# Four gate units by chunk at the start of a two-block kernel, and mixed inputs in tiles of their own

## The chip, the cores and the metric

The kernel runs on one core of a Trainium2 chip (trn2). The metric is the device time of one execution in microseconds (us), median of the runs shown.

## The reference, cut to what matters

Two blocks over 512 tokens of width 1024 in float32. The change touches the first stage of the first block: a norm, the token shift, six mixtures of a token with the one before it, and of these two large products (gate g and reads r, 1024 to 2048) and two small ones for the hidden layers of the low-rank parts (1024 to 64).

```python
h = rms_norm(x, a_norm)
xx = token_shift(h) - h
lerp = lambda j: h + xx * mu[j]
xr, xw, xk, xv, xa, xg = (lerp(j) for j in range(6))
r = xr @ w_in[0]
g = xg @ w_in[3]
hidden_w = jnp.tanh(xw @ w1)      # 64 wide
hidden_a = xa @ a1                # 64 wide
# silu(g) is used at the end of the block, r in its scan
```

Keys and values, k = xk @ w_in[1] and v = xv @ w_in[2], are products of the next stage, which needs their mixed inputs from this one.

## The kernel before, in words

Channels lie on the 128 partitions, the 512 tokens along the free dimension. The width of 1024 is eight chunks (DC), the inner width of 2048 sixteen tiles (IC). Exact float32 products are made from halves: every weight and every input is split into an upper part (type fp32r, a copy that rounds) and a lower part (the whole minus the upper one), and `products` (L140) makes three matmuls for each chunk: upper by upper, upper by lower, lower by upper. One output tile of 128 channels is called a unit here: 8 chunks by 3 matmuls of 512 columns, 24 matmuls. `lerp_phase` (L206 to L511) has 32 of them, N = 32: units 0 to 15 are the gate, 16 to 31 the reads. Unit n uses the PSUM bank 2 + n % 4 (JOBS = 4) and the slot n % 2 of a ring of two weights (RING = 2), each slot with raw, upper and lower part of 128 x 1024.

Each engine has its own program, in an order written out by hand, tied by semaphores:
- SP loads x, a piece of the constants, the parameters, two weights, the first hidden weights, the rest of the constants (L243 to L255), then weight after weight. The load of weight n waits until the slot's weight before it is split (L239). The second hidden weights wait for the first hidden product (L264). From unit 20 on SP also stores finished reads.
- ScalarE squares x for the norm, makes the upper half of each weight (`split`, L299), of each mixed input (`hi`, L304), and the part (1 - mu) h of the gate's and decay's mixtures (`kept`, L311). In the loop over units (L335) it waits for unit n, makes the upper half of weight n + 2, and takes the tanh of the bank (or copies it, for the reads).
- VectorE sums the squares (L463), makes the lower halves of the weights (`split`, L439, through L151), the normed h (L418), the mixed inputs (`whole` L443, `shifted` L421, `lerps` L427), their lower halves (`lo`, L453), and per gate unit the product of the bank and its tanh (L494), which frees the bank.
- GpSimd prepares eight small parameter tiles of 128 x 16 (L285) and, when the gate's inputs are done, the eight differences xx of neighbouring tokens (L288), 128 x 511 each.
- TensorE: units 0 and 1 run side by side chunk by chunk as the inputs appear (`pair_by_chunk`, L388), then unit 2, the first hidden product (`hiddens`, L393, 8 float32 products), unit 3, units 4 and 5, the second hidden product, units 6 to 15. Then units 16 and 17 by chunk, since the reads' mixed inputs are only made then, in the same tiles x_hi and x_lo that the gate used: ScalarE's first write of them waits for gate unit 15 (L308). Units 18 to 31 follow.

The order of VectorE ahead of its loop (L471 to L482): the gate's inputs chunk by chunk, eight one-column instructions for xx (L478), the lower halves of weights 2 and 3, the decay's eight mixed inputs (`lerps(0)`), and a wait for the first hidden product. The two hidden products read their mixed inputs from the gate's output tile (`tmp`, L215), so the gate's results can only be written after those are used. The mixed inputs of keys and values (e = 8 to 23) are made beside units 4 to 11, two chunks a unit (L499).

```python
            pair_by_chunk(0, 0)
            job(2)
            hiddens(0)
            job(3)
```

Of the kernel before, what the change touches and what calls it, by code (L numbers as in the profile page):

```python
# [163 lines left out]
def program(nc, ins, out):  # L164
    with ExitStack() as top:
# [16 lines left out]
        with ExitStack() as right:  # L182
# [13 lines left out]
            with ExitStack() as left:  # L196
                K["lerp"] = {n: pair(left, f"lerp_{n}", DC) for n in "kv"}
                K["r_all"] = nc.dram_tensor("r_all", (IC, P, T), F32).ap()
                K["hidden"] = sbt(left, "hidden", [P, T])
                lerp_phase(K)  # L200
                rwkv_phase(K)
# [4 lines left out]
def lerp_phase(K):  # L206
# [4 lines left out]
    with ExitStack() as ctx:  # L211
# [3 lines left out]
        tmp = [gate[:, 0:DC, :], gate[:, DC:2 * DC, :]]  # L215
        h = x
        x_hi, x_lo = K["pair"](ctx, "xg", DC)
        raw, w_hi, w_lo = (K["sbt"](ctx, "g_" + n, [P, RING, DC * P], t) for n, t in
                           (("raw", F32), ("hi", F32R), ("lo", F32R)))
        full = K["sbt"](ctx, "lerp_full", [P, 2, T])  # L220
# [6 lines left out]
        block = ctx.enter_context(nc.Block())  # L227
        mu = V["a_mu"].rearrange("p (j c) -> p j c", j=6)
# [4 lines left out]
        SPLIT = [(name, j) for name in "gkvr" for j in range(DC)]  # L233
        pairs = {"g": (x_hi, x_lo), "r": (x_hi, x_lo), **lerp}

        @block.sync
        def _(sp):
            def load(n):
                need(sp, S("wlo"), n - RING + 1)  # L239
                sp.dma_start(raw[:, n % RING, :], ins["w_g" if n < IC else "w_r"][n % IC])\  # L240
                    .then_inc(S(f"w{n % RING}"), 16)
# [8 lines left out]
            for n in range(RING):  # L250
                load(n)
# [9 lines left out]
            for n in range(RING, N):  # L261
                load(n)
                if n == JOBS:
                    sp.wait_ge(S("hid_mm"), 1)  # L264
                    sp.dma_start(wl[:, :, :], ins["lora1"][:, :, LORA:P]).then_inc(S("wl"), 16)
                if n >= IC + JOBS:
# [8 lines left out]
        def _(pool):  # L275
# [3 lines left out]
            for n, name in enumerate("gw"):  # L279
                pool.tensor_scalar(rest[:, n, :], mu[:, MU[name], :], -1.0, 1.0, ALU.mult, ALU.add)\  # L280
                    .then_inc(S("rest"), 1)
            for n, (name, a, b) in enumerate((("a_w0", 0.5, 0.0), ("a_a0", 0.5, 0.0), ("a_ka", 0.5, 0.0),
# [8 lines left out]
        def _(act):  # L291
# [7 lines left out]
            def split(n):  # L299
                act.wait_ge(S(f"w{n % RING}"), 16 * (n // RING) + 16)  # L300
                need(act, S("g_mm"), n - RING + 1)
                act.activation(w_hi[:, n % RING, :], raw[:, n % RING, :], ACT.Copy).then_inc(S("whi"), 1)  # L302

            def hi(e):  # L304
                name, j = SPLIT[e]
                act.wait_ge(S("lerp_full"), e + 1)
                if name == "r" and j == 0:
                    act.wait_ge(S("g_mm"), IC)  # L308
# [24 lines left out]
            for j in range(DC):  # L333
                kept(1, j)
            for n in range(N):  # L335
                act.wait_ge(S("g_mm"), n + 1)
                if n == IC - 1:
                    hi(3 * DC)
                    hi(3 * DC + 1)
                if n + RING < N:  # L340
                    split(n + RING)
                if n == 2:
                    act.wait_ge(S("hid_mm"), 1)
                    act.activation(hidden[0:LORA, :], bank[1][0:LORA, :], ACT.Tanh).then_inc(S("hid"), 1)
                if n == 6:
                    act.wait_ge(S("hid_mm"), 2)
                    act.activation(hidden[LORA:P, :], bank[1][LORA:P, :], ACT.Copy).then_inc(S("hid"), 1)
                if n < IC:
                    need(act, S("gate"), n - 1)
                    act.activation(thg[:, n % 2, :], bank[2 + n % JOBS][:, :], ACT.Tanh, scale=0.5).then_inc(S("thg"), 1)  # L350
                    if n >= JOBS and n < JOBS + DC:
                        hi(DC + 2 * (n - JOBS))
                        hi(DC + 2 * (n - JOBS) + 1)
# [7 lines left out]
                if n == IC - 1:  # L361
                    for e in range(3 * DC + 2, 4 * DC):
                        hi(e)

        @block.tensor
        def _(pe):
# [4 lines left out]
            def job(n, ks=range(DC)):  # L371
# [8 lines left out]
                at = n % RING  # L380
                m = products(pe, bank[2 + n % JOBS][:, :], w_hi[:, at, ks[0] * P:], w_lo[:, at, ks[0] * P:],
# [4 lines left out]
            def pair_by_chunk(n, first):  # L386

                for k in range(DC):  # L388
                    pe.wait_ge(S("lerp_lo"), first + k + 1)
# [12 lines left out]

            pair_by_chunk(0, 0)
            job(2)
            hiddens(0)
            job(3)
            for n in range(JOBS, IC):
                job(n)
                if n == JOBS + 1:
                    hiddens(1)  # L410
            pair_by_chunk(IC, 3 * DC)
            for n in range(IC + 2, N):
# [2070 lines left out]
```

## Time and profile before

| | us |
|---|---|
| runs shown | 2048.4, 2050.85, 2056.65 |
| median | 2050.85 |
| the profiled execution | 2047.91 |
| its span | 2045.9 |
| matmul time of TensorE in the span | 1886.3 (92%) |
| last matmul of `lerp_phase` starts at | 235.53 |

The profile describes one execution. Times in it count from the start of its span. Engines are named PE (TensorE matmuls), PEld (its weight loads), DVE (VectorE), ACT (ScalarE), POOL (GpSimd) and SP (SyncE, which issues the DMAs). PEclk is the share of the full clock that TensorE was granted.

### The profile page before, as it was taken

Reading aid. Unit: us, or ns where it says so; the run is one execution under the profiler, and the core shown is the slowest. Engines: PE = TensorE matmul, PEld = TensorE weight load, DVE = VectorE, ACT = ScalarE, POOL = GpSimd, SP = SyncE. Lnnn points to the kernel's source line nnn. Section 1 sums busy time; section 2 is a strip of 40 time slices with the busy share of each in tenths; the row PEclk is TensorE's granted clock in tenths of the full one; section 3 lists DMA queues with packets and bytes.
Section 4 is the critical chain, followed back from the end, with each engine's and each line's share of the span. In section 5 each row is a group of like instructions: output and inputs, shape, how many; then the busy total and the mean of one; then the engine's idle time right before and its main releaser. Section 6 shows DMA issues by size and latency. Waiting matters only on the chain.

```text
span 2045.9 us, 43870 instructions
## 1 busy us (share of the span) xinstructions
PE 1886.3 (92%) x18912; PEld 1475.6 (72%) x18912; DVE 1253.5 (61%) x1787; ACT 884.2 (43%) x1368; POOL 294.1 (14%) x282
## 2 busy tenths in 40 slices
PE   4999779999999999899999999999888699999997
PEld 3677657676777767578888888887665478888885
DVE  6572168787777777544555554546557677787522
ACT  5342255646656466433222222334445354444321
POOL 3000033543535444400000000000000000000000
PEclk9999889999999999999999999999999799999998
DMA  3224311111111111143322223322110032223331
GB/s 123 78 83 139 104 42 45 42 45 41 46 30 42 45 42 39 43 151 97 103 94 94 102 93 101 96 93 73 52 42 21 21 114 98 97 93 103 91 93 64
DMA packets 51454, 154.15 MB, mean 75 GB/s; under 512 B 8512, under 2 KB 11072, under 8 KB 51264
## 3 DMA queue, kind: packets, MB, share of 16 engines
q1 hardware_dynamic: 51264, 151.35, 22.8%
q8 instruction: 151, 2.47, 0.5%
q14 instruction: 39, 0.32, 0.1%
HBM read 145.04 MB, written 6.29 MB: 74 GB/s over the span
## 4 chain that ended last, share of the span: by engine, by line
PE 51%; DVE 4%; ACT 1%; issue 0%; DMA 0%; DVEq 0%; ACTq 0%
PE bank L1653 15%; PE bank L1654 15%; PE bank L1652 15%; PE bank L1740 1%; PE bank L1741 1%; PE bank L1742 1%; DVE room L2364 0%; PE bank L1777 0%; DVE room L2331 0%; PE bank L1760 0%; PE bank L1821 0%; PE bank L1812 0%; PE bank L1723 0%; PE bank L1788 0%; PE bank L1785 0%
## 5 line engine op out<-in xcount | busy, mean ns | idle before, releaser
L1859 ACT ACTIVATE w_hi<-raw 128x1024 fp32r<-128x1024 f32 (+2 forms) x195 | 197.8, 1015 | 499.5 <-PE bank L1654 457.0
L1652 PE MATMUL bank<-h_hi,w_hi 128*128 128x512 f32 x896 | 349.8, 390 | 0.0
L1654 PE MATMUL bank<-h_hi,w_lo 128*128 128x512 f32 x896 | 348.6, 389 | 0.0
L1653 PE MATMUL bank<-h_lo,w_hi 128*128 128x512 f32 x896 | 348.6, 389 | 0.0
L151 DVE TENSOR_TENSOR w_lo<-raw,w_hi 128x1024 fp32r<-128x1024 f32 (+2 forms) x202 | 236.2, 1170 | 155.2 <-ACT w_hi L1859 154.7
L1652 PEld LDWEIGHTS bank<-h_hi,w_hi 128*128 128x128 f32 x896 | 168.2, 188 | 35.7 <-issue 0.7
L1653 PEld LDWEIGHTS bank<-h_lo,w_hi 128*128 128x128 f32 x896 | 168.2, 188 | 35.5 <-issue 0.7
L1654 PEld LDWEIGHTS bank<-h_hi,w_lo 128*128 128x128 f32 x896 | 168.2, 188 | 34.9
L144 PE MATMUL bank<-xg_hi,g_hi 128*128 128x512 f32 x256 | 104.4, 408 | 21.6 <-DVE g_lo L151 11.8
L814 ACT ACTIVATE swapT<-invT 64x256 f32<-64x256 f32 x192 | 79.8, 415 | 83.3 <-DVE invT L1367 41.1
L1634 POOL TENSOR_SCALAR room<-room 128x512 f32<-128x512 f32 x4 | 3.5, 884 | 696.7 <-ACT room L1928 696.7
L145 PE MATMUL bank<-xg_lo,g_hi 128*128 128x512 f32 x256 | 102.8, 402 | 0.0
L146 PE MATMUL bank<-xg_hi,g_lo 128*128 128x512 f32 x256 | 102.7, 401 | 0.0
L151 DVE TENSOR_TENSOR g_lo<-g_raw,g_hi 128x1024 fp32r<-128x1024 f32 x32 | 40.7, 1276 | 91.5 <-ACT g_hi L302 91.5
L1652 PE MATMUL bank<-y_hi,w_hi 128*128 128x512 f32 x224 | 87.7, 391 | 2.3 <-PEq L134 1.3
L1000 PEld LDWEIGHTS bank<-inv,LA 64*64 64x64 f32 x2560 | 46.9, 134 | 59.4 <-issue 59.4
L1653 PE MATMUL bank<-y_lo,w_hi 128*128 128x512 f32 x224 | 88.9, 397 | 0.0
L1654 PE MATMUL bank<-y_hi,w_lo 128*128 128x512 f32 x224 | 88.4, 395 | 0.0
L1347 DVE TENSOR_TENSOR low<-bank,con 128x512 f32<-128x512 f32 x80 | 55.1, 689 | 45.0 <-PE bank L1000 44.9
L1352 DVE TENSOR_TENSOR invT<-invT,bank 128x512 f32<-128x512 f32 x80 | 55.1, 688 | 40.3 <-PE bank L1012 40.3
L144 PEld LDWEIGHTS bank<-xg_hi,g_hi 128*128 128x128 f32 x256 | 50.0, 195 | 39.5 <-DVE xg_lo L151 13.9
L1000 PE MATMUL bank<-inv,LA 64*64 64x64 f32 x2560 | 56.3, 224 | 23.6 <-DVE inv L1356 17.1
(389 smaller groups left out, 4301.3 us busy)
## 6 DMA issues: line engine op xcount, KB each, us to landing
raw<-in_w_conv SPq DMA_DIRECT2D x64, 512.0 KB, 3.2
raw<-in_w_up SPq DMA_DIRECT2D x44, 512.0 KB, 3.2
raw<-in_w_out SPq DMA_DIRECT2D x32, 512.0 KB, 3.8
raw<-in_w_in SPq DMA_DIRECT2D x20, 512.0 KB, 3.2
g_raw<-in_w_g SPq DMA_DIRECT2D x16, 512.0 KB, 3.2
g_raw<-in_w_r SPq DMA_DIRECT2D x16, 512.0 KB, 3.8
w_k<-in_w_k SPq DMA_DIRECT2D x16, 512.0 KB, 4.1
w_v<-in_w_v SPq DMA_DIRECT2D x16, 512.0 KB, 3.6
```

The lines of the kernel that those rows point to most:

```text
L144: pe.matmul(out, w_hi[:, w], x_hi[:, k, :], start=(first and n == 0), stop=False)
L145: pe.matmul(out, w_hi[:, w], x_lo[:, k, :], start=False, stop=False)
L146: m = pe.matmul(out, w_lo[:, w], x_hi[:, k, :], start=False, stop=(last and n == len(ks) - 1))
L151: return dve.tensor_tensor(lo, full, hi.bitcast(F32), ALU.subtract)
L814: act.activation(swapT[rows[1 - j], :, :], invT[rows[j], 1, :, :], ACT.Copy).then_inc(S("swap"), 1)
L1000: m = pe.matmul(X[h][rows[j ^ h], cols(b)], LA[rows[j], h, b, 0, :], inv[rows[j], h, b, :], start=True, stop=True)
L1347: dve.tensor_tensor(low[:, :, :, :], heads(0), over2(C["level_mask"][:, lv * HD:(lv + 1) * HD]), ALU.mult).then_inc(S("low"), 1)
L1352: up = dve.tensor_tensor(invT[:, :, :, :], invT[:, :, :, :], heads(half), ALU.add)
L1652: pe.matmul(to, whi, hi, start=begin, stop=False)
L1653: pe.matmul(to, whi, lo, start=False, stop=False)
L1654: last = pe.matmul(to, wlo, hi, start=False, stop=end)
L1859: act.activation(w_hi[:, g % RING, 0:width], raw[:, g % RAW, 0:width], ACT.Copy).then_inc(S("whi"), 1)
```

## The change

Units 0 to 3 run side by side by chunk: units 2 and 3 one chunk (LAG = 1) behind units 0 and 1. Their weights are loaded at the start. Those of units 2 and 3 lie in tiles `more` over the lower part of the values' input tiles (24 of 32 KB for each partition), with semaphores of their own; GpSimd makes their upper halves. The gate's mixed inputs lie in the keys' input tiles, the reads' in a pair `xr` of their own. The two hidden products' mixed inputs (`mixed_w`, `mixed_a`) lie over `xr`, no longer over the gate's output. The first hidden product comes after unit 5, the second after unit 7. The mixed inputs of reads, values and keys, in this order, are made beside units 8 to 19 (MIX = 8), two chunks a unit, and units 16 and 17 are ordinary units. On VectorE the decay's mixed inputs come ahead of the splits of weights 4 and 5, and the waits for the hidden products in its loop go.

```diff
-                K["lerp"] = {n: pair(left, f"lerp_{n}", DC) for n in "kv"}
+                K["lerp"] = {"k": pair(left, "lerp_k", DC)}
+                K["lerp_v_at"] = -(-nc.sbuf_base // 32) * 32
+                K["lerp"]["v"] = pair(left, "lerp_v", DC)
...
-        tmp = [gate[:, 0:DC, :], gate[:, DC:2 * DC, :]]
-        x_hi, x_lo = K["pair"](ctx, "xg", DC)
+        over = lambda name, at, shape, t: nc.alloc_sbuf_tensor_at(name, shape, t, offset=at)
+        r_at = -(-nc.sbuf_base // 32) * 32
+        pairs = {"g": lerp["k"], "r": K["pair"](ctx, "xr", DC), **lerp}
+        tmp = [over(f"mixed_{n}", r_at + 4 * DC * T * k, [P, DC, T], F32) for k, n in enumerate("wa")]
...
+        more = [over(f"g_{n}_more", K["lerp_v_at"] + 8 * DC * P * k, [P, 2, DC * P], t) for k, (n, t) in
+                enumerate((("raw", F32), ("hi", F32R), ("lo", F32R)))]
+        of = lambda n: [t[:, n - 2, :] for t in more] if n in (2, 3) else [t[:, n % RING, :] for t in (raw, w_hi, w_lo)]
+        MIX, LAG = 8, 1
...
+        weight = lambda n: f"w{n}" if n in (2, 3) else f"w{n % RING}"
+        loads = lambda n: 16 if n < JOBS else 16 * ((n - JOBS) // RING + 2)
...
-        SPLIT = [(name, j) for name in "gkvr" for j in range(DC)]
-        pairs = {"g": (x_hi, x_lo), "r": (x_hi, x_lo), **lerp}
+        SPLIT = [(name, j) for name in "grvk" for j in range(DC)]
...
             def load(n):
-                need(sp, S("wlo"), n - RING + 1)
-                sp.dma_start(raw[:, n % RING, :], ins["w_g" if n < IC else "w_r"][n % IC])\
-                    .then_inc(S(f"w{n % RING}"), 16)
+                if n >= JOBS:
+                    sp.wait_ge(S("wlo"), n - 3 if n < JOBS + 2 else n - 1)
+                sp.dma_start(of(n)[0], ins["w_g" if n < IC else "w_r"][n % IC]).then_inc(S(weight(n)), 16)
...
-            for n in range(RING):
+            for n in range(JOBS):
                 load(n)
...
-            for n in range(RING, N):
-                load(n)
-                if n == JOBS:
+            for n in range(JOBS, N):
+                if n == MIX:
                     sp.wait_ge(S("hid_mm"), 1)
                     sp.dma_start(wl[:, :, :], ins["lora1"][:, :, LORA:P]).then_inc(S("wl"), 16)
+                load(n)
...
+            for n in (2, 3):
+                pool.wait_ge(S(weight(n)), 16)
+                pool.tensor_scalar(of(n)[1], of(n)[0], 1.0, 0.0, ALU.mult, ALU.add).then_inc(S("whi_more"), 1)
...
             def split(n):
-                act.wait_ge(S(f"w{n % RING}"), 16 * (n // RING) + 16)
-                need(act, S("g_mm"), n - RING + 1)
-                act.activation(w_hi[:, n % RING, :], raw[:, n % RING, :], ACT.Copy).then_inc(S("whi"), 1)
+                act.wait_ge(S(weight(n)), loads(n))
+                need(act, S("g_mm"), n - 3 if n < JOBS + 2 else n - 1)
+                act.activation(of(n)[1], of(n)[0], ACT.Copy).then_inc(S("whi"), 1)
...
-                if name == "r" and j == 0:
-                    act.wait_ge(S("g_mm"), IC)
+                if j == 0 and name != "g":
+                    act.wait_ge(*{"r": (S("hid_mm"), 2), "v": (S("g_mm"), JOBS), "k": (S("g_mm"), IC)}[name])
...
+            split(JOBS)
+            split(JOBS + 1)
             for n in range(N):
                 act.wait_ge(S("g_mm"), n + 1)
-                if n == IC - 1:
-                    hi(3 * DC)
-                    hi(3 * DC + 1)
-                if n + RING < N:
+                if JOBS <= n < N - RING:
                     split(n + RING)
-                if n == 2:
+                if n == 6:
-                if n == 6:
+                if n == MIX:
-                    if n >= JOBS and n < JOBS + DC:
-                        hi(DC + 2 * (n - JOBS))
-                        hi(DC + 2 * (n - JOBS) + 1)
...
-                if n == IC - 1:
-                    for e in range(3 * DC + 2, 4 * DC):
-                        hi(e)
+                if MIX <= n < MIX + 3 * DC // 2:
+                    hi(DC + 2 * (n - MIX))
+                    hi(DC + 2 * (n - MIX) + 1)
...
-                at = n % RING
-                m = products(pe, bank[2 + n % JOBS][:, :], w_hi[:, at, ks[0] * P:], w_lo[:, at, ks[0] * P:],
+                _, hi, lo = of(n)
+                x_hi, x_lo = pairs["g" if n < IC else "r"]
+                m = products(pe, bank[2 + n % JOBS][:, :], hi[:, ks[0] * P:], lo[:, ks[0] * P:],
...
-            def pair_by_chunk(n, first):
-
-                for k in range(DC):
-                    pe.wait_ge(S("lerp_lo"), first + k + 1)
+            def two_by_chunk(n, k):
+                if k < DC:
+                    pe.wait_ge(S("lerp_lo"), k + 1)
                     for s in range(2):
                         job(n + s, [k])
...
-            pair_by_chunk(0, 0)
-            job(2)
-            hiddens(0)
-            job(3)
-            for n in range(JOBS, IC):
+            for k in range(DC + LAG):
+                two_by_chunk(0, k)
+                if k >= LAG:
+                    two_by_chunk(2, k - LAG)
+            for n in range(JOBS, N):
+                if n == IC:
+                    pe.wait_ge(S("lerp_lo"), 2 * DC)
                 job(n)
-                if n == JOBS + 1:
-                    hiddens(1)
-            pair_by_chunk(IC, 3 * DC)
-            for n in range(IC + 2, N):
-                job(n)
+                if n in (5, 7):
+                    hiddens((n - 5) // 2)
...
-                dve.wait_ge(S("whi"), n + 1)
-                split_lo(dve, w_lo[:, n % RING, :], raw[:, n % RING, :], w_hi[:, n % RING, :]).then_inc(S("wlo"), 1)
+                dve.wait_ge(*((S("whi_more"), n - 1) if n in (2, 3) else (S("whi"), n + 1 if n < 2 else n - 1)))
+                split_lo(dve, of(n)[2], of(n)[0], of(n)[1]).then_inc(S("wlo"), 1)
...
-            split(0)
-            split(1)
+            for n in range(JOBS):
+                split(n)
...
-            split(RING)
-            split(RING + 1)
             lerps(0)
-            dve.wait_ge(S("hid_mm"), 1)
+            split(JOBS)
+            split(JOBS + 1)
             for n in range(N):
-                if n == IC - 1:
-                    for e in (3 * DC, 3 * DC + 1):
-                        lo(e)
-                        whole(e + 2)
-                if RING <= n < N - RING:
+                if JOBS <= n < N - RING:
                     split(n + RING)
                 if n < IC:
-                    if n == IC // 2:
...
-                if n < 2:
-                    lerps(1, range(n * DC // 2, (n + 1) * DC // 2))
-                if JOBS <= n < JOBS + DC:
-                    e = DC + 2 * (n - JOBS)
+                if n in (JOBS, JOBS + 1):
+                    lerps(1, range((n - JOBS) * DC // 2, (n - JOBS + 1) * DC // 2))
+                if MIX <= n < MIX + 3 * DC // 2:
+                    e = DC + 2 * (n - MIX)
                     whole(e)
                     whole(e + 1)
                     lo(e)
                     lo(e + 1)
-                if n == IC - 2:
-                    whole(3 * DC)
-                    whole(3 * DC + 1)
-                if n == IC - 1:
-                    for e in range(3 * DC + 2, 4 * DC):
-                        lo(e)
-                        if e + 2 < 4 * DC:
-                            whole(e + 2)
```

## Rows read from the trace of the kernel before

**Rows 1.** The page: span, and TensorE's busy time.
```profile
span 2045.9 us, 43870 instructions
...
PE 1886.3 (92%) x18912; PEld 1475.6 (72%) x18912; DVE 1253.5 (61%) x1787; ACT 884.2 (43%) x1368; POOL 294.1 (14%) x282
```

**Rows 2.** Busy time by stretch; columns: length, each engine's (instructions), clock, DMA, GB/s.
```profile
21.10:25.10 4.00, 4.00 (x9) 3.14 (x10) 3.91 (x7) 2.48 (x4) 0.00 (x0) 1.00 0.00 0
25.10:37.00 11.90, 10.28 (x40) 6.74 (x38) 9.32 (x22) 7.85 (x13) 1.43 (x2) 1.00 0.00 0
42.70:49.75 7.05, 7.03 (x25) 5.43 (x25) 7.05 (x8) 0.00 (x0) 2.85 (x2) 0.80 0.24 74
62.50:64.60 2.10, 0.00 (x0) 0.00 (x0) 2.10 (x4) 1.54 (x2) 0.00 (x0) 1.00 0.01 4
64.60:72.10 7.50, 7.47 (x26) 5.95 (x27) 2.30 (x3) 0.00 (x0) 0.00 (x0) 0.77 0.43 140
...
139.10:155.40 16.30, 12.45 (x46) 9.80 (x47) 11.24 (x16) 6.25 (x10) 0.00 (x0) 0.90 0.10 33
155.40:165.30 9.90, 8.09 (x29) 6.17 (x29) 2.45 (x2) 2.98 (x4) 0.00 (x0) 0.83 0.52 159
165.30:236.00 70.70, 70.62 (x312) 58.15 (x310) 14.70 (x12) 19.17 (x26) 0.00 (x0) 1.00 0.41 123
```

**Rows 3.** Waits of TensorE in 0 to 285 us: total, times, longest.
```profile
PE bank L144 <- DVE g_lo L151: 11.8, 4, 5.5
PE bank L144 <- DVE xg_lo L151: 9.8, 6, 6.6
```

**Rows 4.** Timeline of TensorE; columns: start, us, engine, line, operation, operands, count.
```profile
21.10 0.79 PE L144 MATMUL bank<-xg_hi,g_hi 128*128 128x512 f32 x1 [6.63 <-DVE xg_lo L151]
...
49.73 7.08 PE L399 MATMUL bank<-gate,lora_w 128*64 128x512 f32 x16
```

**Rows 5.** Timeline of VectorE, 12 to 36 us.
```profile
12.34 2.38 DVE L151 TENSOR_TENSOR g_lo<-g_raw,g_hi 128x1024 fp32r<-128x1024 f32 x2
17.30 1.42 DVE L418 SCALAR_TENSOR_TENSOR x_in<-x_in,par,thg 128x512 f32<-128x512 f32 x2 [2.59 <-ACT thg L161]
...
20.96 0.75 DVE L423 SCALAR_TENSOR_TENSOR lerp_full<-x_in,par,lerp_full 128x511 f32<-128x511 f32 x1
...
23.03 0.74 DVE L423 SCALAR_TENSOR_TENSOR lerp_full<-x_in,par,lerp_full 128x511 f32<-128x511 f32 x1
...
35.40 0.57 DVE L478 TENSOR_SCALAR xx<-x_in 128x1 f32<-128x1 f32 x8
```

**Rows 6.** The gate's weights, their issue on SP, and the traffic then.
```profile
DMA to landing us min/median/max: 3.2/4.3/7.7
...
4.09 0.93 SPq L240 DMA_DIRECT2D g_raw<-in_w_g  x2
...
13.00:14.00 1.00, 1.00 (x2) 0.00 (x0) 1.00 (x2) 0.38 (x1) 1.00 (x2) 1.00 1.02 425
```

**Rows 7.** Durations (min/median/max ns): a GpSimd copy, and its small instruction.
```profile
L687 POOL TENSOR_SCALAR w_k_hi<-w_k x14: 1047/1057/1479, 294.4 to 762.9; 128x1024 fp32r<-128x1024 f32 x14
...
L285 POOL TENSOR_SCALAR mixpar<-par x8: 214/446/1188, 10.7 to 14.8; 128x16 f32<-128x16 f32 x8
```

**Rows 8.** GpSimd's differences and what met them on VectorE.
```profile
L288 POOL TENSOR_TENSOR xx<-x_in x8: 1038/1039/2022, 35.6 to 43.5; 128x511 f32<-128x511 f32 x8
...
42.59 2.06 DVE L151 TENSOR_TENSOR g_lo<-g_raw,g_hi 128x1024 fp32r<-128x1024 f32 x1
44.57 1.52 DVE L423 SCALAR_TENSOR_TENSOR gate<-x_in,par,gate 128x511 f32<-128x511 f32 x1
...
46.01 0.74 DVE L423 SCALAR_TENSOR_TENSOR gate<-x_in,par,gate 128x511 f32<-128x511 f32 x1
...
46.67 0.74 DVE L423 SCALAR_TENSOR_TENSOR gate<-x_in,par,gate 128x511 f32<-128x511 f32 x1
```

**Rows 9.** Timeline of ScalarE in unit 9.
```profile
101.12 1.06 ACT L302 ACTIVATE g_hi<-g_raw 128x1024 fp32r<-128x1024 f32 x1 [0.53 <-PE bank L146]
```

More of the change, by code:

```diff
@@ L478, in _ @@
                 dve.tensor_scalar(xx[:, j, 0:1], h[:, j, 0:1], -1.0, None, ALU.mult).then_inc(S("xx0"), 1)
-            split(RING)
-            split(RING + 1)
             lerps(0)
-            dve.wait_ge(S("hid_mm"), 1)
+            split(JOBS)
+            split(JOBS + 1)
             for n in range(N):
-                if n == IC - 1:
-                    for e in (3 * DC, 3 * DC + 1):
-                        lo(e)
-                        whole(e + 2)
-                if RING <= n < N - RING:
+                if JOBS <= n < N - RING:
                     split(n + RING)
                 if n < IC:
-                    if n == IC // 2:
-                        dve.wait_ge(S("hid_mm"), 2)
                     dve.wait_ge(S("thg"), n + 1)
```

## The prediction

> **What bounds the kernel now.** The page first: TensorE is busy for 92% of the 2045.9 us span [rows 1], so time lost on it counts, if no other engine is late. The change touches the first 236 us alone, so the next view is the busy time by stretch of that part [rows 2]. A unit is one of the 32 output tiles (16 of the gate, 16 of the reads), 24 matmuls. The last thirteen read units take 70.7 us with 312 matmuls, TensorE without a hole: 5.44 us a unit and 0.227 us a matmul. They end at 236.0. The rest of the stretch has holes. The waits of TensorE say on whom: 5.5 us at most and 11.8 us in all on the lower halves of the weights, 9.8 us on those of the inputs, of which 6.6 us is the wait for the first one [rows 3]. The timeline gives the fixed points: first unit matmul at 21.10 and the first product for a hidden layer, 7.08 us; the second is of the same size [rows 4].
>
> Losses against 24 x 0.2267 = 5.44 us a unit, from [rows 2]:
> - Two gate units by chunk: 21.1 to 37.0 is 15.9 us for 10.9 us of work, 5.0 lost. 1.9 of it is the slow start (9 matmuls in 4.0 us), 3.1 are waits for input chunks.
> - Before unit 2: 5.7 us of hole (37.0 to 42.7), then 7.05 us for the unit, 1.6 more than at full clock.
> - Before unit 4: 2.1 us of hole, then 7.5 us, 2.1 more than 5.44.
> - The first two read units: 16.3 us for 10.9, 5.4 lost.
> - Unit 18: 9.9 us from the end of that pair, 4.5 more than a unit.
>
> Slow start aside these make 3.1 + 7.3 + 4.2 + 5.4 + 4.5 = **24.5 us**. The granted clock is below 1 in the stretches behind the holes (0.80, 0.77, 0.83): part of them ran at 1.2 instead of 2.4 GHz. What came before each fall was a hole or a run of short holes.
>
> **What the change takes away.** (a) Units 0 to 3 run chunk by chunk, 12 matmuls a chunk: 12 x 0.227 = 2.72 us. VectorE gives a chunk every 2.07 us (20.96 to 23.03 [rows 5]). TensorE is the slower one, so the 3.1 us go. (b) Weights 2 and 3 are there from the start, so the hole before unit 2 goes with its cold part, 7.3 us. (c) The hidden product no longer stands between units 3 and 4 with its work on VectorE behind it; 4.2 us go, though something takes the place (below). (d) The reads' inputs have tiles of their own and are made beside units 8 to 11; the pair stage and the hole behind it go, 9.9 us. Unit 16 then waits only for a count reached four units earlier.
>
> **What it adds, at the start.** VectorE now does four weight splits before the norm, where it did two (12.34 to 14.72), and was then idle until 17.30 [rows 5]. The upper halves of weights 2 and 3 come from GpSimd, which is in this place for the first time. Landing: the second weight landed 7.7 us after its issue, which is 12.2 (issues from 4.09 on, 0.93 us for two). DMA moves about 400 GB/s there, so 512 KB more land every 1.3 us: 13.5 and 14.9 [rows 6]. GpSimd takes 1.05 us for the same operation on another weight, VectorE 1.2 us for its own, and one GpSimd instruction of 16 columns took up to 1.19 us instead of 0.21, in the time of VectorE's splits [rows 7]: the two take turns. So from 12.34 on: four VectorE splits of 1.17 start to start and two GpSimd copies of about 0.95 in turn, 4.7 + 1.9 = 6.6, end 18.9; plus 0.2 for the eight small parameter instructions which GpSimd had done by then and now does later. The norm starts at 19.1 to 19.2 instead of 17.30: **+1.9 us**. Ends: 0, if the copies run free (14.9 + 1.05 + 1.2 = 17.2), and 3.8, if a landing is 1 us later and the small instructions take their 0.1 to 0.3 each between VectorE's.
>
> **What it adds, before unit 4.** From here times are without the 1.9. TensorE is busy from 21.10: 9 matmuls to 25.1, 87 x 0.227 more: four units are done at 45.0. VectorE finishes the last input chunk at 35.5 and eight one-column instructions at 36.0 [rows 5]. Then, in its new order, it makes the eight mixed inputs of the first hidden product before the splits of weights 4 and 5. They stand exactly where GpSimd computes the eight differences (from 35.57, 1.04 us each alone). The trace shows what two such operations do to each other: a difference beside a split took 2.02, a split 2.06 instead of 1.2, and the one mixed input that met GpSimd 1.52 instead of 0.74. It started at 44.57 and the next at 46.01: 1.44 apart, against 0.67 alone (46.01 to 46.67) [rows 8]. Before, GpSimd had nearly finished when they came; now all eight meet it. 36.0 + 8 x 1.44 = 47.5. Behind them in VectorE's queue stand the splits of weights 4 and 5 (2.3 us) and the gate of unit 0 (0.7), which frees the bank: 50.5. TensorE waits 50.5 - 45.0 = **5.5 us**, and starts again at a low clock: +1.6 to +2.1 by the two cold units above, **1.8**. Ends of the hole: 0.8 if there is no collision (eight at 0.67 end at 41.4, but ScalarE's half of weight 4 needs unit 0's end, 3.4 us before 45.0; +1.1, two splits, a gate: 45.8), and 7 if a turn costs the sum of both.
>
> The Trainium skill, page "SBUF — State Buffer", section "Who interferes with whom", says that the pair of ports common to VectorE and GpSimd is locked for the whole instruction and the loser fully blocks. By that rule each turn would cost both durations, 1.04 + 0.74 = 1.78 us, and the hole would be 2.7 us longer than in my sum; the rows show 1.44, and the sum goes by them.
>
> **What costs nothing.** Four instead of two weights are issued at the start; the two more stand in front of the first hidden weights and constants in SP's queue, which are needed more than 30 us later. SP waits for the first hidden product before load 8: issued at the end of that product, landed some 4 us later, used by ScalarE after unit 6, 5.4 us later; everything behind it in the queue (load 9 on) is due a unit later still. If that cover went, unit 8 would be late, but the second hidden product and unit 7 stand before it, 12.5 us. The second set of mixed inputs stands beside units 4 and 5, needed after unit 7. The twelve units with input chunks (8 to 19) are what 4 to 11 were: ScalarE has 0.53 us left of 5.44 a unit [rows 9], and a weight may be 3 us late on top before TensorE notices. The values' inputs wait for unit 3, the keys' for unit 15: both long done. The end of the stage and all after it is untouched.
>
> **Sum.** 24.5 - 1.9 - 5.5 - 1.8 = 15.3 us. As a check: 23.0 start, 23.7 four units with the slow start, 5.5 hole, 1.8 cold, 28 x 5.44 = 152.3, 14.2 hidden: 220.5, against 236.0. The profiled execution took 2047.91 us (2.0 outside the span), so it would be 2032.6. The median shown lies 2.9 above that execution. I forecast the median, 2050.85 - 15.3 = **2035.5 us**.
>
> **Rivals.**
> 1. No collision: the eight mixed inputs run at 0.67. The hole is 0.8 and the clock stays: 24.5 - 1.9 - 0.8 = 21.8, 2029. Against it: the one sample that met GpSimd was slowed. For it: one sample only, beside the last of GpSimd's eight. Chance 0.11.
> 2. Full turns of 1.78 us: 2038. For it: 2.06 for a split beside a difference is near to the sum of 1.2 and 1.04; against it the 1.44. The skill's rule named above is this case. Chance 0.12.
> 3. Start and hole both at their dear ends and a further small stall, for instance unit 16 waiting for its inputs because they are not made ahead as the change says, which would give back the 5.4 us of the pair: saving 5 to 10, 2041 to 2046. Chance 0.14.
> 4. Slower: ScalarE's and VectorE's chain of a unit with two input chunks is 4.9 us of 5.44 now. If it grows past 5.44, each of twelve units is paced by it; from 6.7 us a unit on (15.3 / 12 = 1.3 more) the gain is gone, at 7.6 the kernel takes some 2061. Eight units show it at 4.9 without a stall, and GpSimd is silent there. Chance 0.03.
>
> **How the numbers follow.** The forecast has 0.60, its own range 2032 to 2039 (start 0.5 to 3, hole 4 to 7, run to run 2). The 8-in-10 range takes in rival 2 and most of 1 and reaches to the edge of 3: 2028 to 2041. A measurement of this kernel can tell about 0.5%, 10.3 us, from no change. Faster by more than that: forecast, rivals 1 and 2, 0.83. Same: rival 3, 0.14. Slower: 0.03.
>
> **What would show it.** The norm's first VectorE instruction near 19.2. From the first unit matmul no waits for inputs through four units, ending some 26 us later. Mixed inputs on VectorE from about 38, 1.4 us apart, each beside a GpSimd difference; then one TensorE hole of 5 to 6 us, released by VectorE's gate, and a few us at 1.2 GHz behind it. After that a unit every 5.44 us, with no hole at unit 16 or 18; the last ends near 220.5. I am wrong if that hole is under 2 or over 8 us, if the first matmul comes after 25, or if another hole opens from unit 5 on.

## The result, and the profile after

The changed kernel takes 2036.01 us (median of eight runs, 2032.24 to 2042.27), the kernel before 2051.64 us (eight runs, 2048.4 to 2056.65). The ratio is 0.9932 with a 95% interval of 0.9918 to 0.9947: 15.6 us less, where 15.3 us less had been forecast.

The page of the changed kernel says little; its span is only 6.6 us shorter than that of [rows 1], because its profiled execution was one of the longer of the eight (2041.11 us):

```profile
span 2039.3 us, 43871 instructions
...
PE 1888.7 (93%) x18912; PEld 1480.4 (73%) x18912; DVE 1260.3 (62%) x1787; ACT 883.0 (43%) x1366; POOL 298.2 (15%) x284
```

The stage that was changed has to be read by itself. Its end is the copy of the last read unit, in ScalarE's timeline: first the kernel before, then the changed one. It comes 15.49 us earlier.

```profile
235.96 0.60 ACT L360 ACTIVATE thg<-bank 128x512 f32<-128x512 f32 x1 [4.84 <-PE bank L146]
```

```profile
220.47 0.60 ACT L369 ACTIVATE thg<-bank 128x512 f32<-128x512 f32 x1 [4.84 <-PE bank L146]
```

Busy time by stretch of the changed kernel answers to [rows 2] (columns as there):

```profile
22.60:28.40 5.80, 5.80 (x14) 4.54 (x15) 5.67 (x9) 3.73 (x6) 0.00 (x0) 1.00 0.00 0
28.40:47.50 19.10, 19.09 (x84) 15.44 (x82) 17.59 (x27) 12.26 (x19) 10.45 (x8) 1.00 0.01 1
47.50:51.70 4.20, 0.00 (x0) 0.00 (x0) 4.20 (x5) 0.00 (x0) 0.70 (x1) 1.00 0.16 42
51.70:59.10 7.40, 7.34 (x25) 5.92 (x26) 1.80 (x3) 1.20 (x2) 0.00 (x0) 0.77 0.32 118
100.00:154.40 54.40, 54.40 (x242) 45.05 (x241) 43.94 (x59) 28.54 (x41) 0.00 (x0) 1.00 0.33 105
154.40:220.50 66.10, 66.03 (x292) 54.34 (x290) 16.62 (x16) 18.88 (x26) 0.00 (x0) 1.00 0.42 127
```

The rows show four units without a hole (98 records, with those at the edges), then one hole of 4.2 us, a unit of 7.4 us with a granted clock of 0.77, and, in the rows from 100 us on, a full TensorE to the end of the stage. Nothing is left of the read pair. The waits and the timeline of TensorE show that one hole and who ends it:

```profile
PE bank L144 <- DVE lerp_k_lo L151: 8.0, 1, 8.0
PE bank L144 <- DVE gate L496: 4.3, 1, 4.3
```

```profile
22.59 0.79 PE L144 MATMUL bank<-lerp_k_hi,g_hi 128*128 128x512 f32 x1 [8.05 <-DVE lerp_k_lo L151]
...
51.76 0.47 PE L144 MATMUL bank<-lerp_k_hi,g_hi 128*128 128x512 f32 x1 [4.27 <-DVE gate L496]
```

VectorE's timeline of the changed kernel, against [rows 5]: the norm begins at 18.80 instead of 17.30, behind two splits of 1.6 us each. The eight mixed inputs take 11.38 us, which is 1.42 us each, and the splits of weights 4 and 5 and the gate stand behind them:

```profile
15.69 3.19 DVE L151 TENSOR_TENSOR g_lo_more<-g_raw_more,g_hi_more 128x1024 fp32r<-128x1024 f32 x2 [0.94 <-POOL g_hi_more L294]
18.80 1.40 DVE L427 SCALAR_TENSOR_TENSOR x_in<-x_in,par,thg 128x512 f32<-128x512 f32 x2
...
37.37 11.38 DVE L432 SCALAR_TENSOR_TENSOR mixed_w<-x_in,par,mixed_w 128x511 f32<-128x511 f32 x8
48.67 2.35 DVE L151 TENSOR_TENSOR g_lo<-g_raw,g_hi 128x1024 fp32r<-128x1024 f32 x2
50.94 2.68 DVE L496 SCALAR_TENSOR_TENSOR gate<-thg,bank 128x512 f32<-128x512 f32 x4
```

GpSimd's timeline beside it: its eight differences take 11.15 us, from 37.05 to 48.2. In the kernel before they took 10.0 us, and in experiment 1 below, where next to nothing meets them, 8.0 us.

```profile
13.66 3.02 POOL L294 TENSOR_SCALAR g_hi_more<-g_raw_more 128x1024 fp32r<-128x1024 f32 x2 [2.85 <-DMA g_raw_more<-in_w_g]
...
37.05 11.15 POOL L301 TENSOR_TENSOR xx<-x_in 128x511 f32<-128x511 f32 x8 [15.16 <-DVE lerp_k_lo L151]
```

### The profile page after: what moved, and what is told of

Same layout as the page of the kernel before. It is cut to its first block, busy times and chain, and to the rows that moved or that the text cites. A ratio compares the mean times of both kernels' runs of the same rounds, so it can differ in the third digit from the quotient of the medians.

```text
span 2039.3 us, 43871 instructions
## 1 busy us (share of the span) xinstructions
PE 1888.7 (93%) x18912; PEld 1480.4 (73%) x18912; DVE 1260.3 (62%) x1787; ACT 883.0 (43%) x1366; POOL 298.2 (15%) x284
## 4 chain that ended last, share of the span: by engine, by line
PE 51%; DVE 4%; ACT 1%; issue 0%; DVEq 0%; ACTq 0%
PE bank L1647 15%; PE bank L1648 15%; PE bank L1646 15%; PE bank L1734 1%; PE bank L1736 1%; PE bank L1735 1%; DVE room L2358 0%; PE bank L1771 0%; DVE room L2325 0%; PE bank L1754 0%; PE bank L1815 0%; PE bank L1806 0%; PE bank L1717 0%; PE bank L1782 0%; PE bank L1779 0%
## 5 line engine op out<-in xcount | busy, mean ns | idle before, releaser
L151 DVE TENSOR_TENSOR g_lo<-g_raw,g_hi 128x1024 fp32r<-128x1024 f32 x30 | 36.6, 1224 | 81.4 <-ACT g_hi L315 81.4
L1006 PEld LDWEIGHTS bank<-invT,low 64*64 64x64 f32 x1280 | 45.1, 134 | 33.3 <-issue 33.3
L2090 DVE TENSOR_TENSOR x<-x,bank 128x512 f32<-128x512 f32 x32 | 21.9, 686 | 73.7 <-PE bank L1648 68.5
L315 ACT ACTIVATE g_hi<-g_raw 128x1024 fp32r<-128x1024 f32 x30 | 31.7, 1059 | 82.7 <-PE bank L146 82.7
L1006 PE MATMUL bank<-invT,low 64*64 64x64 f32 x1280 | 54.9, 223 | 10.4 <-DVE low L1341 10.4
```

The lines of the kernel that those rows point to most:

```text
L151: return dve.tensor_tensor(lo, full, hi.bitcast(F32), ALU.subtract)
L315: act.activation(of(n)[1], of(n)[0], ACT.Copy).then_inc(S("whi"), 1)
L1006: m = pe.matmul(X[h][rows[j], cols(TB + b)], low[rows[j ^ h], h, b, :], right, start=True, stop=True)
L2090: dve.tensor_tensor(x[:, n, :], x[:, n, :], bank[at + n % wide(tag)][:, :], ALU.add)\
```

## The experiments

The theory: TensorE sets the pace of the stage, VectorE's queue makes the one hole that is left, and it does so because the mixed inputs and GpSimd's differences take turns (when both are due, one waits while the other works). The effect of an edit is read from the end of the stage; the times of whole runs scatter by more than most of the effects (last part of this section).

**1. The mixed inputs later.** The eight mixed inputs of the decay are taken out from ahead of the splits.

```diff
-            lerps(0)
             split(JOBS)
             split(JOBS + 1)
             for n in range(N):
...
+                if n == JOBS - 1:
+                    lerps(0)
                 if n in (JOBS, JOBS + 1):
```

> The changed kernel, but the decay's eight mixed inputs are made on VectorE after the gate of unit 3, no longer ahead of the splits of weights 4 and 5. Theory (VectorE's queue, stretched by turns with GpSimd's differences, made the 4.3 us hole before unit 4 and the slow clock behind it): four units end at 47.5, the splits at 47.5 and the gate of unit 0 at 48.1, a hole of about 0.7 us, no fall of the clock; unit 4 starts 3.6 us earlier and takes 5.4 instead of 7.4 us. The stage's last unit ends near 214.9 instead of 220.5, the time is 5.6 us under the changed kernel (about 2030.5). Rival (the hole has another cause, weight 4 or the bank): the end stays at 220.5. Rival (the clock falls there whatever happens): the end is near 217.

Measured: median 2030.91 us, ratio to the kernel before 0.9907 (0.9887 to 0.9928). The stage ends at 215.24. TensorE and VectorE, timelines of this kernel:

```profile
48.17 0.47 PE L144 MATMUL bank<-lerp_k_hi,g_hi 128*128 128x512 f32 x1 [0.90 <-DVE gate L495]
```

```profile
47.35 2.69 DVE L495 SCALAR_TENSOR_TENSOR gate<-thg,bank 128x512 f32<-128x512 f32 x4
49.95 5.38 DVE L432 SCALAR_TENSOR_TENSOR mixed_w<-x_in,par,mixed_w 128x511 f32<-128x511 f32 x8
```

Busy time by stretch, unit 4 of this kernel:

```profile
48.20:53.70 5.50, 5.50 (x25) 4.56 (x26) 5.37 (x9) 1.12 (x2) 0.00 (x0) 1.00 0.41 138
```

The hole is 0.90 instead of 4.27 us, unit 4 starts 3.6 us earlier, and the clock did not fall: its stretch takes 5.5 us at a granted clock of 1.00. Neither weight 4 nor the bank had another cause for more than these 0.90 us. The same eight instructions take 5.38 us once the differences are done (GpSimd's end at 45.2 here). Both rivals fall. From the start of unit 4 to the end of the stage the changed kernel took 168.71 us and this one 167.07, so the fall of the clock costs 1.6 us there.

**2. The differences later.** VectorE's order stays, GpSimd waits.

```diff
-                pool.wait_ge(S("lerp_lo"), DC)
+                pool.wait_ge(S("lerp"), DC)
```

> The changed kernel, but GpSimd's eight differences wait for the decay's eight mixed inputs to be done, so that they no longer run side by side. Theory (the two engines take turns): the mixed inputs start 0.67 us apart instead of 1.42 and end near 42.8 instead of 48.8; the differences then meet the splits of weights 4 and 5, which take about 2.0 us each instead of 1.2; the gate of unit 0 ends near 50, the hole is about 2.5 us, the stage ends at 217 to 219. Rival (mixed inputs slow for another reason, such as ScalarE's half or TensorE's reading beside them): they keep 1.42 us, end stays at 220.5 or comes later.

Measured: median 2029.96 us, ratio 0.9905 (0.9874 to 0.9936), stage end at 214.94.

```profile
37.49 5.37 DVE L432 SCALAR_TENSOR_TENSOR mixed_w<-x_in,par,mixed_w 128x511 f32<-128x511 f32 x8
43.89 3.20 DVE L151 TENSOR_TENSOR g_lo<-g_raw,g_hi 128x1024 fp32r<-128x1024 f32 x2 [1.03 <-ACT g_hi L315]
```

Below are GpSimd's timeline of this kernel, and the durations (min/median/max ns) of the mixed inputs, first in the changed kernel, then in this one:

```profile
42.94 10.03 POOL L301 TENSOR_TENSOR xx<-x_in 128x511 f32<-128x511 f32 x8 [20.95 <-DVE mixed_w L432]
```

```profile
L432 DVE SCALAR_TENSOR_TENSOR mixed_w<-x_in,par,mixed_w x8: 1266/1521/1522, 37.4 to 47.2; 128x511 f32<-128x511 f32 x8
```

```profile
L432 DVE SCALAR_TENSOR_TENSOR mixed_w<-x_in,par,mixed_w x8: 741/744/746, 37.5 to 42.1; 128x511 f32<-128x511 f32 x8
```

In the same place, with ScalarE and TensorE at work beside them as before, the mixed inputs start 0.67 us apart: it was GpSimd. The two splits now meet the differences and take 3.20 us instead of 2.35, less than the 4.0 expected. The end came earlier than the 217 to 219 expected, because the hole was 1.74 us instead of 2.5 and the clock did not fall behind it.

**3. Two units, then two.** Only TensorE's order is undone.

```diff
-            for k in range(DC + LAG):
+            for k in range(DC):
                 two_by_chunk(0, k)
-                if k >= LAG:
-                    two_by_chunk(2, k - LAG)
+            for k in range(DC):
+                two_by_chunk(2, k)
```

> The changed kernel with its four weights, but TensorE takes units 0 and 1 by chunk and then units 2 and 3 by chunk. Theory (the restart before unit 4 is set by VectorE's queue at 51.7, not by TensorE): the first pair ends at 38.5, the second at 49.4 instead of 47.5, the hole shrinks from 4.3 to 2.3 us and unit 4 starts at 51.7 as before; the stage ends at 219.5 to 220.5, no difference in time. Rival (running four side by side is itself what brings the gain): the stage ends 2 to 3 us later, 222.5 to 223.5.

Measured: median 2035.2 us, ratio 0.9929 (0.9902 to 0.9956), stage end at 220.73. The waits for input chunks are back (9.5 us in all, of which 8.3 is the wait for the first chunk). The four units end at 49.84 instead of 47.49, the hole is smaller by nearly as much, and unit 4 starts when VectorE lets it:

```profile
PE bank L144 <- DVE lerp_k_lo L151: 9.5, 4, 8.3
PE bank L144 <- DVE gate L496: 2.2, 1, 2.2
```

```profile
52.04 0.60 PE L144 MATMUL bank<-lerp_k_hi,g_hi 128*128 128x512 f32 x1 [2.21 <-DVE gate L496]
```

The end moves by 0.3 us, as does the first matmul (22.87 instead of 22.59); two executions of the changed kernel differ by 1.5 us (run 8 below). The rival, an end 2 to 3 us later, falls. In the changed kernel the side by side order brings nothing that shows. What is gained ahead of unit 4 must then come from the weights that are ready and the hidden product that has moved; neither was tried alone.

**4. The reads' part alone.** Built on the kernel before: only the tiles, the order of the mixed inputs and the read units are changed.

```diff
-        SPLIT = [(name, j) for name in "gkvr" for j in range(DC)]
-        pairs = {"g": (x_hi, x_lo), "r": (x_hi, x_lo), **lerp}
+        SPLIT = [(name, j) for name in "grvk" for j in range(DC)]
+        MIX = 8
+        pairs = {"g": lerp["k"], "r": (xr_hi, xr_lo), **lerp}
...
-            for n in range(JOBS, IC):
+            for n in range(JOBS, N):
+                if n == IC:
+                    pe.wait_ge(S("lerp_lo"), 2 * DC)
                 job(n)
...
-            pair_by_chunk(IC, 3 * DC)
-            for n in range(IC + 2, N):
-                job(n)
...
```

> The kernel before with one part of the change: the gate's mixed inputs in the keys' tiles, the reads' in a pair of their own, made beside units 8 to 11, and units 16 and 17 as ordinary units. Start, weights and hidden products as before. Theory (this part is worth the 5.4 us of the pair stage and the 4.5 us of unit 18): the stage ends near 226.1 instead of 236.0, time 9.9 us under the kernel before, near 2041.7. Rival (the holes only move, because inputs or weights come late beside units 12 to 19): the stage ends at 230 or later.

Measured: median 2041.95 us, ratio 0.9965 (0.9949 to 0.9981), stage end at 224.82, 11.1 us under [rows 2]'s 236.0. Busy time by stretch in this kernel, the hole before unit 4, unit 4, and the time of some eighteen units from 120 us on:

```profile
62.70:64.90 2.20, 0.05 (x2) 0.00 (x1) 2.20 (x4) 1.54 (x2) 0.00 (x0) 1.00 0.01 4
64.90:70.35 5.45, 5.45 (x24) 4.48 (x25) 2.27 (x3) 0.00 (x0) 0.00 (x0) 1.00 0.55 192
...
120.00:219.30 99.30, 99.30 (x440) 82.23 (x439) 47.58 (x57) 38.92 (x54) 0.00 (x0) 1.00 0.40 126
```

There is no hole from 120 on. From the end of unit 15 to the end of the stage this kernel takes 86.95 us (137.87 to 224.82) and the kernel before 96.76 (139.20 to 235.96): 9.8 us, where 9.9 were expected. The rest of the 11.1 is chance. The hole before unit 4 is the one of [rows 2], 2.15 us in the waits of both, but the clock fell behind it there and not here. So this part carries 9.8 of the 15.5 us, and all that happens before the end of unit 15 carries 5.7. The median is only 7.2 us under that of the kernel before in the same series (2049.16 us), and the profiled execution was the fastest of nine, so the 9.8 us rest on the stage and not on the time of whole runs.

**5. Two, then two, with a free VectorE.** The edits of 1 and 3 together.

> Both edits of the first and third experiment: the decay's mixed inputs after the gate of unit 3, and TensorE takes units 0 and 1, then units 2 and 3. Theory (with VectorE's queue free, TensorE's own order decides): the first pair is again paced by VectorE until 38.6, the second ends at 49.5, unit 4 starts at 49.6 without a hole instead of 48.2, the stage ends at 216.2 to 216.8 instead of 215.2: side by side is worth 1 to 1.5 us, and only here. Rival (the order never matters): 215.2 again. Rival (it is worth the whole 3.1 us of waits): 218.

Measured: median 2031.0 us, ratio 0.9906 (0.9881 to 0.993), stage end at 216.68 instead of 215.24; there is no wait for the gate in this kernel. The order is worth 1.4 us, as expected (one profile of this kernel), and only once VectorE's queue does not hide it. The median of the whole run does not show it.

**6. The splits of weights 2 and 3 behind the second chunk**, on top of 1, to win back the start.

```diff
-            for n in range(JOBS):
+            for n in range(2):
                 split(n)
...
                 lo(j)
+                if j == 1:
+                    split(2)
+                    split(3)
```

> The first experiment's kernel (decay's mixed inputs after the gate of unit 3), and on VectorE the splits of weights 2 and 3 stand behind the second input chunk, no longer ahead of the norm. Theory (the two splits and GpSimd's copies are what delays the start by 1.5 us; TensorE, slower than VectorE by 0.65 us a chunk, has room for 2.4 us of them later): the norm starts at 17.3, the first unit matmul at 21.1, units 2 and 3 start near 25.8, a wait of at most 1 us for the third chunk; four units end at 45.5 to 46.5, the stage ends at 213 to 214.3 instead of 215.2, time near 2029.5. Rival (the delay only moves from the start to units 2 and 3): the first matmul at 21.1 but the end at 215.2. Rival (the holes at chunk 2 bring the slow clock back): the end at 216 or later.

Measured: median 2030.24 us, ratio 0.9902 (0.9884 to 0.9921), but the stage ends at 216.43, later than in 1. VectorE's timeline shows the norm back at 17.31, and what happened further on:

```profile
17.31 1.47 DVE L427 SCALAR_TENSOR_TENSOR x_in<-x_in,par,thg 128x512 f32<-128x512 f32 x2 [2.32 <-ACT thg L161]
...
43.32 3.66 DVE L151 TENSOR_TENSOR g_lo<-g_raw,g_hi 128x1024 fp32r<-128x1024 f32 x2 [5.02 <-ACT g_hi L315]
```

```profile
47.70:55.00 7.30, 7.28 (x25) 5.86 (x26) 7.05 (x11) 1.16 (x2) 0.17 (x1) 0.77 0.21 72
```

The second fence is the stretch of unit 4. TensorE is 1.5 us ahead, so the splits of weights 4 and 5 come earlier and now meet the differences (3.66 instead of 2.36 us), the hole is 2.19 us, and the clock falls behind it. The second rival of the expectation holds (the slow clock is back), for a hole in another place than it named. The start itself is won back: the first unit matmul comes at 21.16, so the two splits were what had delayed it.

**7. Both meetings avoided.** Edit 6 without edit 1, and the differences behind the splits of weights 4 and 5.

```diff
-                pool.wait_ge(S("lerp_lo"), DC)
+                pool.wait_ge(S("wlo"), JOBS + 2)
```

> The changed kernel with two edits: the splits of weights 2 and 3 stand behind the second input chunk, and GpSimd's differences wait for the splits of weights 4 and 5, so that they meet neither the mixed inputs nor these splits. Theory (the start's delay and the two meetings of VectorE and GpSimd are all that is left between this stage and a full TensorE): norm at 17.3, first unit matmul at 21.1, mixed inputs 0.67 us apart, the splits 1.2 us each, a hole of about 0.9 us before unit 4 and no slow clock behind it; the stage ends at 212.5 to 214, 6.5 to 8 us ahead of the changed kernel, time near 2029. Rival (the differences are then late for the second hidden layer's mixed inputs): a hole before the second hidden product, end at 216 or later.

Measured: median 2031.01 us, ratio 0.9892 (0.9874 to 0.9909), stage end at 213.71.

```profile
38.22 5.37 DVE L432 SCALAR_TENSOR_TENSOR mixed_w<-x_in,par,mixed_w 128x511 f32<-128x511 f32 x8
43.51 2.35 DVE L151 TENSOR_TENSOR g_lo<-g_raw,g_hi 128x1024 fp32r<-128x1024 f32 x2
```

```profile
46.60 0.47 PE L144 MATMUL bank<-lerp_k_hi,g_hi 128*128 128x512 f32 x1 [1.07 <-DVE gate L499]
```

The stage is as forecast, 6.8 us ahead of the changed kernel, with a hole of 1.07 us and no fall of the clock behind it. The time of the run is not: 2 us over the forecast.

**8 to 10. What the rest of the kernel does.** The changed kernel, the kernel of 7 and that of 1 once more each.

> The changed kernel unaltered, on the same chip as the one above. Theory: the stage again ends within 1.5 us of 220.5 (the slow start of TensorE differs by up to that), while the time of all that follows differs by up to 10 us from one execution to another, as the code there is the same: its spread goes with the stretches of lower granted clock. Rival (the change itself makes the later stages slower): they take 1818 us again, not 1808 to 1815.

> The kernel of e7 again, unaltered. Theory (its stage ends 7 us ahead of the changed kernel's, and the 1820 us that followed in its profile were the scatter of the clock in the later stages): the stage ends at 213 to 214.5 again, what follows takes 1808 to 1818 us, median 2028 to 2031. Rival (ending the stage earlier costs something later): what follows takes 1820 us again, median 2031 or more.

> The kernel of e1 again, on the same chip as the one above. Theory: the stage ends at 214.5 to 215.5, what follows takes 1808 to 1818 us, median 2029 to 2032.

Measured: 8 has a median of 2034.81 us (ratio 0.9917, 0.9902 to 0.9933) and a stage end of 221.97, 9 has 2031.65 us (0.9897, 0.9876 to 0.9918) and 213.57, 10 has 2028.37 us (0.9897, 0.9878 to 0.9917) and 215.20. Run 8 ends its stage 1.5 us later than the first profile of the same kernel: it started 0.3 us later, and behind its hole 13 matmuls of unit 4 ran slowly instead of 8, so that from the start of unit 4 to the end of the stage it took 169.87 instead of 168.71 us. The slow start, which the expectation had named as the cause, was shorter in run 8. In run 10 the hole is 1.75 us where the same kernel had 0.90 in experiment 1: its slow start was shorter, so that the splits came earlier and met the differences (3.21 us), but the gate came at the same time and unit 4 started at 48.11.

After the stage comes the same code in all. These are busy times by stretch, from 8 us behind the stage's end to about 20 us before the end of the span, of the changed kernel, of 8, and of 7:

```profile
228.50:2019.00 1790.50, 1686.69 (x18086) 1324.32 (x18087) 1133.82 (x1626) 789.40 (x1234) 277.48 (x256) 0.98 0.22 70
```

```profile
230.00:2011.00 1781.00, 1679.74 (x18091) 1318.92 (x18092) 1131.23 (x1626) 789.33 (x1234) 280.92 (x256) 0.98 0.22 71
```

```profile
221.70:2014.00 1792.30, 1690.13 (x18088) 1326.48 (x18089) 1133.00 (x1626) 789.34 (x1234) 277.19 (x256) 0.97 0.22 70
```

The same matmuls (some 18,090 records in each) take 1686.7 us in one execution of the changed kernel and 1679.7 us in another, 7.0 of the 9.5 us between the two stretches. Span less stage end is 1818.8 and 1809.1 us, 9.7 apart for one and the same program. The mean granted clock of the whole span goes the same way, 0.975 and 0.978, and 0.974 for 7, where it is 1820.3. That answers the 6.6 us of the page: 15.5 us were won in the stage, and this execution lost 8.9 us against the profile before in code that the change does not touch, which another execution did not lose. Run 9 had 1816.2 us (2029.8 less 213.57) and run 10 1809.6 us. So the rival of 8, that the change makes the later stages slower, falls. Run 9 settles less: 1816.2 lies in the 1808 to 1818 of its theory, but its median of 2031.65 lies over the 2028 to 2031 of the theory, where its rival had it. Run 10 is within its theory but for the median, which is 0.6 us under the 2029 to 2032 expected.

Left open: the kernel of 7 ends the stage 1.6 us before that of 1, and its times are not better (medians over both series 2031.3 us of ten runs and 2030.4 us of eleven). Both its profiles have a long rest, 1820.3 and 1816.2. Whether that is scatter or a price of the earlier end was not settled. Both are faster than the changed kernel, whose median over its thirteen runs is 2035.4 us; the 5.0 us of the kernel of 1 agree with the 5.2 us that its stage ends earlier.

## Why the prediction was right

The forecast was 2035.5 us and 2036.01 us was measured; its own sum for the end of the stage was 220.5, and 220.47 was measured. Point by point:

- **The reads' part, 9.9 us.** Right. No hole is left at units 16 and 18, and the part alone shows it (experiment 4).
- **The hole before unit 2, 7.3 us, and the one before unit 4, 4.2 us.** The first is gone. The second is gone with its cause too, and the new hole below stands in its place. The profile shows both; neither was tried alone.
- **The start, +1.9 us.** The first unit matmul came at 22.59, +1.5, and experiments 6 and 7 take these 1.5 us back by moving the two splits. The landings were guessed well (13.5 for a copy that began at 13.66). The two copies took 1.04 and 2.00 us and the splits 2.05 and 1.21, in turns; the small parameter instructions after them, up to 1.18 us long themselves, cost VectorE nothing that shows.
- **The four units.** Forecast 23.7 us with a slow start of 1.9; measured 24.9 (22.59 to 47.49). The slow matmuls went on for some 6 instead of 4.0 us (14 in the first 5.8 us), a term 1.0 us too small; the rest of the 1.2 is the end of the last matmul. The length of the slow start differs from one execution to another: in run 8, the same kernel, they went on for 4.0 us and the four units took 24.1 (22.93 to 47.03). The 26 us that the prediction gives among its signs do not fit its own 23.7.
- **The hole before unit 4, 5.5 us.** The mechanism is shown by experiments 1 and 2. Measured 4.3: against the sum, both with the start of +1.5, TensorE came 1.0 us later and VectorE 0.2 us earlier. The 0.8 us that the prediction gave for the case of no collision was right too: 0.90, 1.07 and 0.99 us in experiments 1, 7 and 9, in which neither the mixed inputs nor the splits met the differences. The turns of 1.44 us, taken from a single instruction that had met GpSimd [rows 8], were 1.42.
- **The slow clock behind it, 1.8 us.** Measured 1.6 (168.71 against 167.07 us from the start of unit 4 on, experiment 1), and 2.8 in run 8.
- Start, four units and hole are off by -0.4, +1.2 and -1.2 us and cancel nearly. The agreement to 0.1 us is luck: a second execution of the same kernel ended its stage 1.5 us later. The agreement to 1 or 2 us is not. That the median is met to 0.5 us is luck too, since the time of whole runs scatters by more.
- **The side by side order, 3.1 us of waits taken away.** Here the prediction's account was wrong, though its sum was right: it booked 3.1 us as won and 5.5 us as a new hole. Experiment 3 gives waits back and the end moves by 0.3 us, since unit 4 waits for VectorE either way: what is won there only makes the hole longer. A wait removed ahead of a later one on the same engine is worth nothing as long as the end of the later one stays where it is. Experiment 5 shows what the order is worth without that later wait, 1.4 us and not 3.1.

Rival 1 (no collision) falls by the 11.38 us of the mixed inputs. Rival 2, full turns of 1.78 us, falls as well, by the 1.42 us. The Trainium skill ("SBUF — State Buffer", section "SBUF: two separate sides") says that of a VectorE instruction with two SBUF inputs and a GpSimd instruction that reads SBUF, the first to start has the shared pair of ports for the whole instruction, and the other is fully blocked. The trace agrees that the two hold each other up (1.42 us apart instead of 0.67), but not with the sum of the durations: even 0.67 us start to start for the one and 1.0 for the other (experiment 1, the differences alone) make 1.67. Rival 3 did not happen in the stage. Rival 4 falls: from 100.0 to 154.4, ten units with input chunks beside them run at 5.44 us each.

## What to carry to other kernels

Before a step is moved forward in an engine's queue, look who else works at its new place and who stands behind it: here a move of eight instructions into GpSimd's time made 5.4 us into 11.4, and a change of one line (experiment 2) won 5.5 us of stage time. Measure a local change by the time at which its stage ends; the whole run scattered by 10 us over code that was the same. Waits in a row on one engine don't add up: ask which comes last before counting one as won.

## What the runs showed of the hardware

- VectorE's instructions with two SBUF inputs and GpSimd's on SBUF take turns: a mixed input of 0.74 us took 1.52 (median of eight) beside the differences, two splits of 2.35 took 3.20 to 4.01. Others did not suffer. The eight one-column instructions took 0.57 us in the changed kernel, where the differences began beside them, and in experiment 2, where GpSimd was silent. Four gate instructions, with one SBUF and one PSUM input, took 2.68 us beside the differences (experiment 2) and 2.68 without them (changed kernel).
- Before unit 4 a hole of about 2.2 us in TensorE's work went both ways. Behind holes of 0.9, 1.0, 1.1, 1.7 and 1.75 us there the clock stayed at 2.4 GHz in all five runs. Behind 2.15 us it fell to 1.2 GHz in the kernel before and stayed in experiment 4; behind 2.19, 2.21, 4.27 and 5.07 us it fell each time. A fall made eight or nine matmuls of unit 4 slow (0.43 instead of 0.23 us apart) and cost 1.6 us in four kernels; in run 8 it was 13 matmuls and 2.8 us.
- TensorE's first matmuls, behind 6.6 to 8.5 us of waiting, run 0.43 us apart. How long this lasts differs from one execution to another, also of the same kernel: 6.1 and 4.0 us in the two of the changed kernel, 5.3 and 3.2 in those of experiment 1, 2.7 in experiment 2. The column of the granted clock shows 1.00 all the same (14 slow matmuls in 5.8 us); why is not shown, and the spacing of the matmuls is the safer reading.
